# Moving the cross-attention of two tiles and the step from six to nine gather buffers to an earlier place in an expert-retrieval decoder step

## The reference, cut to what matters

```python
def block(xt):                                     # 128 tokens
    q = (xt @ w_pq).reshape(PEER_BLOCK, PEER_HEADS, 2, D_HALF)
    s = jnp.einsum('thcd,hckd->thck', q, sub_keys)
    s1, i1 = lax.top_k(s[:, :, 0], PEER_TOPK)      # 16 of 128 keys, twice
    s2, i2 = lax.top_k(s[:, :, 1], PEER_TOPK)
    ...                                            # best 16 of the 16 x 16 pairs: idx, gate
    h = jnp.einsum('td,thkd->thk', xt, u_tab[idx])
    a = jax.nn.gelu(h, approximate=False) * gate
    return jnp.einsum('thk,thkd->td', a, v_tab[idx])
```

```python
xp = xp + memory_attention(rms_norm(xp, g_cross[l]), mk, mv, w_cq[l], w_co[l])
...
xp = xp + peer_ffn(rms_norm(xp, g_ffn[l]), *peer_w)
```

## Time and profile before

| what | value |
|---|---|
| median of 3 runs | 1737.28 us (1735.56 to 1740.85) |
| the profiled execution | 1740.85 us, span from first to last instruction 1739.1 us |
| granted TensorE clock, mean over the span | 0.863 of 2.4 GHz |
| busy over the span | PE 75%, DVE 67%, ACT 47%, POOL 37% |
| moved | 655.25 MB, mean 377 GB/s |
| gathers (L606) | 576, of which the first is issued at 207.0 us, the last at 1706.7 us |

### The profile page before, as it was taken

How to read it: one execution, slowest core, us unless ns; L and a number is a source line. 1 busy time by engine, 2 the same in 40 slices (tenths; PEclk the granted TensorE clock), 3 DMA queues, 4 the chain that set the end, 5 groups by cost and what they waited for, 6 DMA issues and landing times.

```text
span 1739.1 us, 21552 instructions
## 1 busy us (share of the span) xinstructions
PE 1301.0 (75%) x7059; PEld 474.8 (27%) x7059; DVE 1172.2 (67%) x2760; ACT 812.2 (47%) x2335; POOL 644.5 (37%) x583
## 2 busy tenths in 40 slices
PE   7999878787898876667777766667677667666765
PEld 3454423342343321213232111111111111111110
DVE  2444567877666677777776677777766677677664
ACT  1434356775344455445554455455444445444433
POOL 0000134334443344333444444444454444444441
PEclk9999988898999888988888788888888887888866
DMA  9433689999999999999999999999999999999995
GB/s 357 154 121 146 253 346 389 359 379 369 415 417 421 393 409 420 389 411 394 399 397 368 422 421 421 421 422 421 421 421 421 421 421 421 422 421 421 417 421 211
DMA packets 97473, 655.25 MB, mean 377 GB/s; under 512 B 12416, under 2 KB 17152, under 8 KB 20544
## 3 DMA queue, kind: packets, MB, share of 16 engines
q0 software_dynamic: 83056, 604.28, 85.0%
q1 hardware_dynamic: 14304, 49.59, 7.6%
HBM read 650.62 MB, written 4.19 MB: 377 GB/s over the span
## 4 chain that ended last, share of the span: by engine, by line
DMA 46%; PE 24%; DVE 11%; ACT 10%; issue 7%; POOL 1%; ACTq 0%; SPq 0%; DVEq 0%; POOLq 0%
DMA R<-in_peer_uv,R 45%; PE ps L1925 8%; PE ps L1472 5%; DVE R L1410 4%; PE ps L1449 3%; ACT L875 2%; ACT R L884 2%; PE ps L1731 2%; ACT R L879 2%; POOL R L606 1%; ACT R L875 1%; PE ps L1457 1%; DVE R L1240 1%; DVE R L1243 1%; DVE R L1241 1%
## 5 line engine op out<-in xcount | busy, mean ns | idle before, releaser
L1925 PE MATMUL ps<-R 64*64 64x512 f32 x4608 | 747.9, 731 | 404.8 <-ACT R L884 403.8
L606 POOL DMA_INDIRECT R<-in_peer_uv,R x576 | 642.5, 1115 | 996.5 <-PE ps L1925 801.3
L1410 DVE CUSTOM_DVE_ANT_0 R<-R 128x1024 f32<-128x1024 f32 x576 | 700.6, 1225 | 404.5 <-DMA R<-in_peer_uv,R 400.8
L875 ACT ACTIVATE R<-R 128x1 f32<-128x1 f32 x576 | 116.1, 202 | 629.1 <-DVE R L1410 627.7
L1925 PEld LDWEIGHTS ps<-R 64*64 64x64 f32 x4608 | 138.4, 150 | 757.9 <-ACT R L884 663.2
L884 ACT ACTIVATE R<-R 128x64 f32<-128x64 f32 x576 | 200.4, 348 | 53.2 <-ACT R L879 0.4
L1731 PE MATMUL ps<-A,R 128*128 128x256 f32 (+1 forms) x640 | 219.2, 467 | 0.7 <-ACT R L767 0.7
L879 ACT ACTIVATE R<-R 128x1 f32<-128x1 f32 x576 | 169.7, 295 | 20.9
L1731 PEld LDWEIGHTS ps<-A,R 128*128 128x128 f32 (+1 forms) x640 | 92.8, 196 | 260.1 <-issue 256.9
L1472 PE MATMUL ps<-A,R 128*128 128x512 f32 (+1 forms) x256 | 100.4, 544 | 0.0
L1449 PE MATMUL ps<-R 128*128 128x256 f32 (+2 forms) x384 | 94.9, 403 | 0.0
(11 more groups left out here) (271 smaller groups left out, 881.9 us busy)
## 6 DMA issues: line engine op xcount, KB each, us to landing
R<-in_peer_uv,R POOLq DMA_INDIRECT x576, 16.0
A<-in_w_pq SPq DMA_DIRECT2D x8, 1024.0 KB, 10.4
A<-in_w_in SPq DMA_DIRECT2D x3, 2048.0 KB, 22.4
R<-in_w_out SPq DMA_DIRECT2D x5, 1024.0 KB, 8.9
R<-in_w_out SPq DMA_DIRECT2D x1, 3072.0 KB, 10.0
R<-in_w_mkv SPq DMA_DIRECT2D x2, 1024.0 KB, 9.3
R<-in_x_promptT SPq DMA_DIRECT2D x4, 512.0 KB, 8.6
x_res<-in_x_prompt SPq DMA_DIRECT2D x4, 512.0 KB, 11.3
```

The costliest lines, as they stand in the source:

```text
L606: pool.indirect_dma_start(slots[slot_of[g]], None, I["peer_uv"][:, :], bass.IndirectOffsetOnAxis(ap=idx[:, b % 4, k:k + 1], axis=0)).then_ ...
L875: act.activation(hgelu[:, b % 2, col], hdot[:, b % 2, col], ACT.Gelu).then_inc(gelu_ready, 1)
L1410: dve.tensor_tensor_reduce(u, u, xn(t), 1.0, 0.0, ALU.mult, ALU.add, hdot[:, b % 2, k:k + 1]).then_inc(u_used, 1)
L1925: ins = pe.matmul(bank(2 * (t % 2) + q)[rows], diag[tokens, g % DIAGS, :], v_rows[slot_of[g]][tokens, c * 512:(c + 1) * 512], start=first, ...
```

## The change

Three things are moved, and no arithmetic is added or removed.

1. Slots. The table by least recent use is replaced by three rings: five slots up to g = 9, six up to g = 207, nine from g = 208 (before: from g = 270). The wait for `l_add` stands before gather 208 alone.
2. Places. Preparation, cross-attention and query products of tiles 3 and 4 move from g = 204 to 267 to g = 142 to 202, into tile 1's experts; those of tile 2 move up by 2 to 6 experts. The row norm of tile 3's expert mixer moves from 237 to 242. The output pieces are set at (77, 80, 83, 90, ...), and the final norms of tiles 0 and 1 go from blocks 18 and 19 to blocks 12 and 14.
3. Banks. Since tile 1 accumulates in banks 2 and 3, tiles 2, 3 and 4 are all prepared in banks 0 and 1, and waits are adapted.

```diff
-SLOT_PHASES = ((0, (0, 1, 2, 3, 4)), (10, (0, 1, 2, 3, 4, 5)), (270, tuple(range(9))))
+FIRST_SLOTS, SLOTS, MORE_SLOTS = 5, 6, 9
+SLOTS_FROM = 2 * FIRST_SLOTS
+MORE_FROM = SLOTS_FROM + 33 * SLOTS
...
-        slot_of = list(slot_table())
+        slot_of = [g % FIRST_SLOTS if g < SLOTS_FROM else (FIRST_SLOTS + g - SLOTS_FROM) % SLOTS if g < MORE_FROM
+                   else (SLOTS + g - MORE_FROM) % MORE_SLOTS for g in range(BLOCKS * TOPK)]
...
-        PREP_AT = {1: -1, 2: 122, 3: 204, 4: 236}
-        QUERY_AT = {1: 5, 2: 134, 3: 212, 4: 244}
-        CROSS_AT = {1: 8, 2: 138, 3: 216, 4: 248}
-        FFN_AT = {1: 28, 2: 158, 3: 237, 4: 16 * 23 + 2}
+        PREP_AT = {1: -1, 2: 120, 3: 142, 4: 172}
+        QUERY_AT = {1: 5, 2: 128, 3: 149, 4: 179}
+        CROSS_AT = {1: 8, 2: 132, 3: 162, 4: 183}
+        FFN_AT = {1: 28, 2: 152, 3: 16 * 15 + 2, 4: 16 * 23 + 2}
         UNIT_AT = (22, 29, 36, 43, 50, 57)
-        OUT_AT = (75, 79, 83, 89, 93, 97, 103, 107, 111, 117, 121, 125)
+        OUT_AT = (77, 80, 83, 90, 93, 96, 103, 106, 109, 116, 118, 120)
...
-        FINAL_SLOT = {18: 0, 19: 1, 21: 2, 29: 3}
+        FINAL_SLOT = {12: 0, 14: 1, 21: 2, 29: 3}
...
-                    elif slot_of[g] == 5:
+                    elif g == SLOTS_FROM:
                         pool.wait_ge(p_q, 2)
-                    elif slot_of[g] > 5:
+                    elif g == MORE_FROM:
                         pool.wait_ge(l_add, 2 * (TILES - 1))
...
-                act.activation(qcT(t), v3(bank(0 if t == 2 else 2)[:, 0:256], 2), ACT.Copy).then_inc(p_qo, 1)
+                act.activation(qcT(t), v3(bank(2 if t == 1 else 0)[:, 0:256], 2), ACT.Copy).then_inc(p_qo, 1)
...
-            spare = expert_T(1 if t == 3 else 2)
+            spare = expert_T(1 if t in (0, 1, 3) else 2)
...
-                src = ps[:, 0:1024] if t == 2 else ps[:, 1024:2048]
+                src = ps[:, 1024:2048] if t == 1 else ps[:, 0:1024]
...
                     else:
                         pe.wait_ge(p_qo, t - 1)
-                        pe.wait_ge(acc_added, 2)
...
-                a = (0 if t == 2 else 1024) + k * P
+                a = (1024 if t == 1 else 0) + k * P
...
-            out = bank(0 if t == 2 else 2)[:, c * P:(c + 1) * P]
+            out = bank(2 if t == 1 else 0)[:, c * P:(c + 1) * P]
...
-                pe.wait_ge(f_out, 2 * t - 1)
+                pe.wait_ge(f_out, 1 if t == 1 else 3 if t == 2 else 5)
...
                 if first and t == 2:
-                    pe.wait_ge(p_qo, 2)
-                if first and t == 3:
                     pe.wait_ge(p_qo, 4)
```

More of the change, by code:

```diff
@@ L351, in hybrid_step @@
         best_ready, gexp_ready, idx_ready = sem("best_ready"), sem("gexp_ready"), sem("idx_ready")
-        landed = [sem(f"landed{i}") for i in range(len(slots))]
+        landed = [sem(f"landed{i}") for i in range(MORE_SLOTS)]
         gate_ready = sem("gate_ready")
```

## The result

| | before | after |
|---|---|---|
| median of seven runs each, us | 1737.28 (1735.56 to 1744.50) | 1747.87 (1743.51 to 1753.34) |
| ratio, with its 95% interval | 1 | 1.006 [1.004, 1.008] |
| the profiled execution, us | 1740.85 | 1754.49 |

The change makes the kernel 10.4 us slower (0.006 of 1737.28), and the interval of the ratio leaves 1 out. I had forecast 1737 us, and the measured time lies 1.9 us above my range. The profiled execution of after is slower still; what is read from it are differences between places. Single executions far from the rest, as one of e3 at 3633.80 us where the others took 1748.26 to 1753.77, are in no ratio.

What follows compares the result with a forecast made beforehand. The gathers were taken to bound the expert loop; 13.5 us won against 13.0 us of costs gave -0.5 us from the profiled 1740.85, stated as 1737 us from the median 1737.28. The range was 1729 to 1746.

Steps and rivals of the forecast that it cites:

- Nine slots give back 13.5 us: Gathers past g = 208: nine slots cover every lateness, so the 13.5 us lost from 783 to 956 us come back.
- a rival: Later part: the want of cross-attention, not nine slots, makes it clean; included in the forecast, no chance of its own.
- Steps (c) to (g): g = 148 to 199, the moved cross-attention work under six slots: costs of 3.0, 2.0, 1.7, 2.4 and 2.9 us.
- The rule of lateness less 7 us: Six-slot gathers: time from landing to the end of its eight matrix instructions loses its excess over about 7 us.
- The final gains' load and the stores of tiles 0 and 1, are moved but not more: no cost in sum: Final norms' transfers, now under six slots: bytes moved but not more, priced at no cost.
- step (g): Tile 4's output product at 199, on top of the additions at 195: lateness 9.9, cost 2.9 us.
- Step (a): Output pieces at 116, 118 and 120, tile 2's preparation behind: lateness 12.2 where it was 11.2, cost 1.0 us.
- PE's bursts run together: Slower rival, adjoining experts: costs reach 21 us, time 1745; sign: g = 120 to 208 over 18 us longer; chance 0.26.
- The faster rival: Early six-slot stretch takes up the cross-attention of tiles 3 and 4: costs about 6 us, time 1730; chance 0.26.
- The wider cover: Six slots bear 9.5 us of lateness: 3.7 us of costs stay, 9.8 won, 1727.5 us; chance 0.03.
- The last sum of the bounds: Upper bound: threshold 6.8 and nothing covered, costs about 19.6, some 3 more at low clock: +9 us (1746).
- (e): Tile 3's output product at 178, tile 4's products at 179 and 180: cost 1.7 us, 5.2 if nothing is covered.

Runs made afterwards that it cites:

- e3: The changed kernel with nine slots from g = 274 instead of 208; 1750.50 us, ratio to before 1.0051.
- e7: The kernel before with six slots kept up to g = 447, nine from 448 instead of 270; 1740.05 us, ratio 0.9995.
- e1: The changed kernel with the final norms of tiles 0 and 1 back in blocks 18 and 19; 1744.52 us, ratio to before 1.0027.
- e9: The changed kernel with pieces, tile 2 and final norms as before, tiles 3 and 4 six experts later, nine slots from 214; 1738.28 us, ratio to before 0.9988.
- e10: The changed kernel with tile 0's final norm in block 13 (g = 217) instead of block 12 (g = 201); 1743.62 us, ratio to before 1.0022.
- e6: The kernel before with only the last three output pieces moved, to 116, 118 and 120; 1739.33 us, ratio 1.0003.
- e5: The kernel before with only the first nine output pieces at their new places (77 to 109); 1740.30 us, ratio 1.0013.
- e2: The kernel before with the new places of all twelve output pieces alone; 1744.26 us, ratio 1.0016.
- e4: The kernel before with the new places of the output pieces and of tile 2's steps; 1746.16 us, ratio 1.0029.
- e12: The kernel before with the cross-attention of tiles 3 and 4 two experts later (218 and 250), nine slots from 276; 1738.16 us, ratio 0.9987.
- e13: e9 with tile 4's steps and tile 3's cross-attention two experts later; 1743.69 us, ratio to before 1.0019.

## Why the prediction was wrong, step by step

**Nine slots give back 13.5 us: the amount near, the cause wrong.** From 208 to 280 after won 12.3 us, some 10 against the mean of the four profiles with before's places. But the sentence "Past g = 208 the nine slots cover every lateness above, so the 13.5 us come back" does not hold: e3 keeps six slots there and wins 12.5, and e7 loses nothing in its median without the nine. The gain travels with the cross-attention. I had named that as a rival and put it in the forecast, since the sum is the same.

**Steps (c) to (g): right in the mechanism and near in the size.** Together 12.0 us; e1, which holds them without the early final norm, lost 13.2 from g = 134 to 208, e9 8.7, and the six profiles with before's own places 0.1 to 3.7, for no change at all. The lateness of after went to 9.6 at 150 (I had 10.0), 10.2 at 168 (9.0), 8.3 at 180 (8.7), 10.1 at 189 (11.3) and 9.8 at 200 (9.9). The rule of lateness less 7 us can be tried on e1. Against an even 2.48 us for each gather it lost 3.0, 3.4, 3.5, 3.2 and 3.8 us in the stretches from g = 149 to 162, 178, 189, 199 and 214. The greatest lateness of each was 9.7, 10.0, 9.4, 10.1 and 9.6, so the rule gives 2.7, 3.0, 2.4, 3.1 and 2.6: near, and a little short. The net of this core is e9's -2 us against my -1.5; that it is so close is in part luck, since e9's profile lost 8.7 us where the sum had 12.0, and the interval of its time takes in no difference, too.

**"The final gains' load and the stores of tiles 0 and 1, are moved but not more: no cost in sum": this is the step that failed.** I priced the transfers of the final norms and not their 4.06 us of ACT, and step (g) was walked without the norm that stands at g = 201, two experts behind the output product. The runs showed in its place a lateness of 13.2 us where step (g) had 9.9, and a price of 5.7 us by e1 and 6.6 by e10, half or more of the 10.4 (each give or take some 4; by the medians of their sessions 3.4 and 4.3). It was to be had from the material: the table loads are in the earlier trace rows, and block 12 starts at g = 192.

**Step (a): mis-sized.** I gave 1.0 us to the last three pieces, which is near e6's 0.5, and nothing to the first nine and to tile 2's steps. e5 has 2.3 for the nine and e2 2.8 for all twelve (4.9 by the medians), with intervals that reach down to 0.3 and 0; e4, with tile 2, has 5.0 and leaves 1.0 out. The nine stand three experts apart where before had four at 89, 93 and 97. That a piece at the low clock has no room there is the likely reason, and not shown.

The three parts make 5.0 (e4) - 2 (e9) + 5.7 (e1) = 8.7 of the 10.4 us, within what the intervals leave. Of the rivals, *PE's bursts run together* came nearest, in its time (1745), in its sense and by its own sign: from g = 120 to 208 after took 20.3 us longer than before, where the sign was over 18. But it came at another place than those it named, and it takes an ACT that waits behind PE. The faster rival fails by e1 and e9, whose stretch from 134 to 208 cost 13.2 and 8.7 us where it had some 6 for all of the costs. The wider cover fails too: it left 2.7 us for (c) to (g), where these stretches lost 13.2 and 8.7.

Two slips in my prediction change nothing in this. The last sum of the bounds comes to less than it says: with 5.2 in place of 1.7 for (e) and 0.2 more for each of the six, the costs are about 17.7 and not 19.6, and the upper end some 1744. And 422 GB/s stands in the earlier trace rows from the 23rd slice on, not the 24th.

Nothing tried beats before by more than 0.13%: the best are e12 and e9 with 0.9987 and 0.9988, e9's interval takes in 1, and e13, which joined their ideas, was slower.

## What to carry to other kernels

Before moving a step, list what each in-order engine has queued at the new place, the norms and copies too, and look for an instruction by which one engine waits for another's backlog: there the two delays add up. Find out whether a buffer ring or the work around it makes a stretch clean before paying to have the ring earlier, by running the old ring with the new places. And walk every moved piece, not only those nearest to the part that the change is about.

## What the runs showed that I had not expected

The cost of one unchanged piece of code differed with the granted clock from one profiled execution to the next. In after the stretch from 473.0 to 481.2 us was granted 0.61 of the full clock, in e1 the same work from 472.0 to 477.6 us 0.89, and sixteen matrix instructions took 5.35 or 3.62 us. PE had stood idle for 1.40 us before the group ahead in after, for 0.59 in e1, and for 2.63 and 2.62 before the group ahead of that; groups of eight take 1.98 us at the lower of the two levels (1.2 GHz) and 1.09 at the higher (2.4 GHz). With the old order of the pieces the time from the landing of 86 to that of 101 stayed at 39.9 to 41.9 us over eight profiles, with the new one it was 41.4 to 46.0 over eight.
